# Prompt mixer of a two-layer hybrid decoder: five vector jobs of each tile done by POOL in place of DVE

## What is computed

```python
def rglru_mixer(...):                 # convolution, gates, recurrence
    u = conv_b
    for j in range(CONV_W):           # 4 taps
        u = u + xc[:, j:j + T] * conv_w[j]
    r = sigmoid(einsum(ub, rg_wa) + rg_ba); i = sigmoid(einsum(ub, rg_wx) + rg_bx)
    log_a = -RG_C * r * softplus(-rg_lambda)
    a = exp(log_a)
    b = sqrt(-expm1(2.0 * log_a)) * i * u          # 1 - a^2
    h = linear_scan(a, b, h0)
    y = gelu(a_gate) * h                           # the gate polynomial

q = partial_rope(rmsnorm(b_q per head, q_norm), pos)   # head squares
k = partial_rope(rmsnorm(b_k per head, k_norm), pos)

def index_scores(qi, wi, ki):         # decides which 256 keys a row attends to
    dots = einsum('bqhd,bsd->bqhs', qi, ki) * (IDX_DIM ** -0.5)
    return einsum('bqh,bqhs->bqs', wi, relu(dots))
```

## Time and profile before

| | us |
|---|---|
| median of three runs | 4593.22 (4589.61 to 4599.74) |
| the profiled execution | 4589.05, its span 4587.4 |
| prompt mixer, both layers, from the timeline | about 2 x 945 |
| PE busy over the span | 3712.4 (81%) |
| DVE busy | 2138.1 (47%) |
| ACT busy | 1037.1 (23%) |
| POOL busy | 546.9 (12%) |

### The profile page before, as it was taken

The page is one execution under the profiler, slowest core; times in us unless marked ns, Lnnn a source line. Parts: engine busy times, 40 slices in busy tenths (PEclk is TensorE's granted clock), DMA queues, the critical chain, the costliest instruction groups (busy, mean ns, idle before and its releaser), DMA issues.

```text
span 4587.4 us, 52594 instructions
## 1 busy us (share of the span) xinstructions
PE 3712.4 (81%) x17978; PEld 2757.6 (60%) x17978; DVE 2138.1 (47%) x4901; ACT 1037.1 (23%) x2273; POOL 546.9 (12%) x767
## 2 busy tenths in 40 slices
PE   5787778776638999999957787787766389999999
PEld 3555455553324899989835554554433248899898
DVE  1357788715503344344413577787155033443443
ACT  2322333223300211112022333332233002111120
POOL 0100100114120000100001000001141201001000
PEclk9888877556769999999978888775567699999999
DMA  3000000015331111111130000000153311111111
GB/s 121 19 13 14 14 10 8 7 29 168 98 130 60 46 37 56 37 37 56 44 120 20 12 13 15 10 8 7 30 170 96 128 60 47 37 56 37 37 56 49
DMA packets 165855, 230.68 MB, mean 50 GB/s; under 512 B 64562, under 2 KB 130164, under 8 KB 163540
## 3 DMA queue, kind: packets, MB, share of 16 engines
q1 hardware_dynamic: 139892, 166.03, 11.0%
q0 software_dynamic: 25696, 61.29, 4.4%
HBM read 203.74 MB, written 23.50 MB: 50 GB/s over the span
## 4 chain that ended last, share of the span: by engine, by line
PE 62%; issue 11%; DVE 10%; SPq 5%; ACT 4%; DVEq 2%; DMA 2%; POOLq 2%; POOL 1%; ACTq 0%
PE bank L1302 11%; PE bank L1303 11%; PE bank L1304 11%; PE bank L1012 9%; PE bank L1008 4%; PE bank L1110 3%; PE bank L1294 3%; DVE arena L1363 3%; SPq L455 2%; SPq L471 2%; ACT arena L642 1%; PE bank L1094 1%; POOLq L591 1%; DVE arena L1629 1%; SPq L424 1%
## 5 line engine op out<-in xcount | busy, mean ns | idle before, releaser
L1771 DVE TENSOR_TENSOR x_and_hraw<-x_and_hraw,bank 128x512 f32<-128x512 f32 (+1 forms) x576 | 396.4, 688 | 630.6 <-PE bank L1304 630.6
L642 ACT ACTIVATE arena<-bank 128x512 f32<-128x512 f32 (+11 forms) x926 | 356.2, 428 | 1112.6 <-PE bank L1012 335.8
L1012 PE MATMUL bank<-arena 128*128 128x512 f32 (+5 forms) x1440 | 526.3, 521 | 3.5 <-ACT arena L669 2.0
L1363 DVE TENSOR_SCALAR_CACHE_REDUCE arena<-arena,vectors 128x384 bf16<-128x384 f32 (+6 forms) x434 | 500.2, 1152 | 34.4 <-issue 2.5
L1302 PE MATMUL bank<-xT_hi,w_up_hi 128*128 128x364 f32 (+1 forms) x1536 | 506.7, 330 | 3.2 <-DVE vectors L1752 3.2
L1303 PE MATMUL bank<-xT_lo,w_up_hi 128*128 128x364 f32 (+1 forms) x1536 | 506.6, 330 | 0.0
L1304 PE MATMUL bank<-xT_hi,w_up_lo 128*128 128x364 f32 (+1 forms) x1536 | 506.5, 330 | 0.0
L1302 PE MATMUL bank<-w_down_hi,hidden_hi 128*128 128x512 f32 x1152 | 450.4, 391 | 7.5 <-issue 7.5
L1303 PE MATMUL bank<-w_down_lo,hidden_hi 128*128 128x512 f32 x1152 | 449.8, 390 | 0.0
L1304 PE MATMUL bank<-w_down_hi,hidden_lo 128*128 128x512 f32 x1152 | 449.6, 390 | 0.0
L1012 PEld LDWEIGHTS bank<-arena 128*128 128x128 f32 (+1 forms) x1440 | 254.4, 194 | 255.3 <-issue 225.4
(11 more groups left out here) (248 smaller groups left out, 4554.6 us busy)
## 6 DMA issues: line engine op xcount, KB each, us to landing
arena<-in_cache_k SPq DMA_DIRECT2D x256, 128.0 KB, 2.2
arena<-in_cache_v POOLq DMA_DIRECT2D x256, 128.0 KB, 2.4
w_up_landing<-in_w_up SPq DMA_DIRECT2D x32, 1024.0 KB, 7.5
w_down_landing<-in_w_down SPq DMA_DIRECT2D x32, 1024.0 KB, 4.9
arena<-in_w_in SPq DMA_DIRECT2D x16, 1322.0 KB, 17.6
out_projection<-in_w_out SPq DMA_DIRECT2D x16, 512.0 KB, 7.1
out_projection<-y_scratch SPq DMA_DIRECT2D x16, 512.0 KB, 3.6
y_scratch<-arena POOLq DMA_DIRECT2D x18, 256.0 KB
```

The source lines that it names most:

```text
L642: return act.activation(dst, src, ACT.Copy, scale=scale)
L1012: ins = mm(b[:R, o:o + w], xnT[:, c, 0:R], w_in[:, c, c0:c0 + w], start=c == 0, stop=c == 7)
L1363: ts(junk, sc, cf[:R].bitcast(F32), None, ALU.is_ge, ALU.add, accum_out=cnt[:R])
L1771: tt(x, x, b[P - R:P, :], ALU.add).then_inc(s_took, 1)
```

## The change

Five functions go from DVE's program into POOL's: `head_squares`, `conv`, `gelu_inner`, `one_minus_a2` and `index_scores`. POOL does the first three one after the other at the start of a stage, ahead of `rstd(s+1)`; `one_minus_a2` behind the issues of the key and value stores; the index scores of all chunks after that. DVE's reduction over 64 columns becomes six additions of halves on POOL, and each multiply-and-add of DVE (one instruction) becomes a multiply by a column of constants and an addition (two), with an area `taps` for what lies between. A new semaphore `s_scored` tells DVE's `top_sign` that the scores of its tile are complete; `recurrence` now waits for `s_u` itself. DVE keeps the two memsets of the sample tile, in `sample_states`. `stored(s_ybst)`, which used to follow the store of the attention output at once, comes after `stored(s_kst)`, and that comes after `one_minus_a2`. PE's, ACT's and SP's programs are unchanged.

```diff
+                def head_squares(t):
+                    R = rows(t)
+                    pool.wait_ge(s_evac, A_AT[l, t, "G2"] + 1)
+                    pool.tensor_tensor(sq[:R], hb[:R, 0:12, :], hb[:R, 0:12, :], ALU.mult)
+                    pool.drain()
+                    for w in (32, 16, 8, 4, 2):
+                        pool.tensor_tensor(sq[:R, :, 0:w], sq[:R, :, 0:w], sq[:R, :, w:2 * w], ALU.add)
+                        pool.drain()
+                    pool.tensor_tensor(small[:R, 32:44], sq[:R, :, 0], sq[:R, :, 1], ALU.add)
+                    pool.drain()
+                    inv_root(small[:R, 20:32], small[:R, 32:44], 1.0 / 64).then_inc(s_krs, 1)
...
+                def conv(t):
...
+                    for h in range(2):
...
+                        pool.tensor_scalar(uo, xs(0), convw[:, 0, h:h + 1], vecs[:, h:h + 1], ALU.mult, ALU.add)
+                        for j in range(1, 4):
+                            pool.tensor_scalar(tap[j % 2], xs(j), convw[:, j, h:h + 1], None, ALU.mult)
+                            pool.drain()
+                            ins = pool.tensor_tensor(uo, uo, tap[j % 2], ALU.add)
+                        pool.drain()
+                    pool.sem_inc(s_u, 1)
...
+                def index_scores(t, c):
...
+                            pool.tensor_scalar(src, src, wi, None, ALU.mult)
+                            pool.drain()
+                            pool.tensor_tensor(dst, dst, src, ALU.add).then_inc(s_idx, 1)
+                        pool.drain()
...
                     if s < TILES:
                         t, R = s, rows(s)
-                        pool.wait_ge(s_kssq, T(l, t) + 1)
-                        inv_root(small[:R, 20:32], small[:R, 32:44], 1.0 / 64).then_inc(s_krs, 1)
+                        head_squares(t)
+                        conv(t)
+                        gelu_inner(t)
                     if s + 1 < TILES:
                         rstd(s + 1)
...
+                        one_minus_a2(t)
                         stored(s_kst)
+                        if attends(s - 1) is not None:
+                            stored(s_ybst)
+                        if 2 <= t < NT:
+                            for c in range(len(chunks(width(t)))):
+                                index_scores(t, c)
                         pool.wait_ge(s_ossq, T(l, t) + 1)
...
-                        if h == 0 and P_:
-                            head_squares(s)
                         if h == 1:
-                            if P_:
-                                conv(s)
+                            if s == NT:
+                                sample_states()
                             if N_:
                                 norm_x(s + 1)
-                        if h == 2 and P_:
-                            gelu_inner(s)
...
-                        if h == 2 and P_:
-                            one_minus_a2(s)
...
-                        if h in (4, 5) and 2 <= s < NT and h - 4 < len(chunks(width(s))):
-                            index_scores(s, h - 4)
```

More of the change, by code:

```diff
@@ new lines, in one_minus_a2 @@
+                def one_minus_a2(t):
+                    R = rows(t)
+                    pool.wait_ge(s_thr, T(l, t) + 1)
+                    pool.tensor_tensor(hh[:, :, 0:R], la[:, :, 0:R], la[:, :, 0:R], ALU.mult)
+                    pool.drain()
+                    pool.tensor_scalar(hh[:, :, 0:R], hh[:, :, 0:R], 1.0, None, ALU.add)
+                    pool.drain()
+                    pool.tensor_tensor(b2[:, :, 0:R], b2[:, :, 0:R], hh[:, :, 0:R], ALU.mult)
+                    pool.drain()
+                    pool.tensor_scalar(b2[:, :, 0:R], b2[:, :, 0:R], 1e-18, None, ALU.max).then_inc(s_b2, 1)
@@ new lines, in index_scores @@
+                def index_scores(t, c):
+                    c0, w = chunks(width(t))[c]
+                    for i in range(4):
+                        pool.wait_ge(s_evac, A_AT[l, t, f"i{c}.{i}"] + 1)
+                        src, dst = rl[:, (IDX0[l, t] + 4 * c + i) % 2, 0:w], score[:, t % 3, c0:c0 + w]
+                        wi = wca[:, t % 2, i:i + 1]
+                        if i == 0:
+                            pool.tensor_scalar(dst, src, wi, None, ALU.mult).then_inc(s_idx, 1)
+                        else:
+                            pool.tensor_scalar(src, src, wi, None, ALU.mult)
+                            pool.drain()
+                            pool.tensor_tensor(dst, dst, src, ALU.add).then_inc(s_idx, 1)
+                        pool.drain()
+                    if c == len(chunks(width(t))) - 1:
+                        d = score[:, t % 3, t * P:(t + 1) * P]
+                        pool.tensor_tensor(d, d, cs("bias"), ALU.add).then_inc(s_scored, 1)
@@ L540, in _ @@
+                pool.wait_ge(s_w, NW * 16 * (l + 1))
                 rstd(0)
```

82 lines of the change are left out of this document (23 added, 59 removed).

## The result

The changed kernel takes 4724.48 us (median of four runs, 4720.35 to 4727.32) against 4595.67 for the kernel before in the same four rounds. The ratio is 1.0281, with an interval of 1.0263 to 1.0299. The profiled execution is at 4723.3 us, 134 us above the one of before. The forecast was slower, 4686 us, with a range up to 4775; the direction and the place were right, and the loss came out about 40 us larger than the sum.

The account below looks back on a forecast made before the run. PE was taken to bound each stage's body, behind a serial head that POOL's chain would lengthen. Terms gave +46.6 us a layer, +93 for two; 4589.05 became 4682, plus 4.2 for the median: 4686 us, range 4605 to 4775.

Parts of the forecast that it names:

- The bound: Prompt mixer stages 1 to 7: serial head, then body set by PE; only shortening the head shortens the stage.
- the port in full and somewhat dearer operations: Outcome band 4710 to 4770 us: POOL fully waits out DVE neighbours and its operations cost somewhat more; chance 0.20.
- the port in full: Rival: beside `heads`, POOL operations wait out DVE neighbours fully, +1.7 us per stage, 4713; chance 0.20 together with dearer operations.
- The chain on POOL: Stage head: squares, root, convolution, polynomial and `rstd` in series before `norm_x`, 19.6 us; 17 to 21 us had chance 0.42.
- eight with one input (0.31 each): POOL's convolution: eight one-input operations at 0.31 us each, within its 6.5 us.
- The neighbour on DVE: POOL's convolution beside DVE's nine `heads` operations: 2 us added for disturbance, between 0 and 3.7.
- the dear rival: POOL fixed costs of 0.4 us per operation, chain 25 to 29 us, 4833 at 28.8; dearer still had chance 0.11.
- What costs nothing: Stage body: 1 - a^2 (about 2.6 us) and index scores (14 us) on POOL are covered; up to +36 if not.
- 2.3 expected: Stage 7, head 6: PE's 2.26 us wait for ACT, behind DVE's maximum, goes: -2.3 us.
- 4.5 us of relief: Stage 8, where DVE sets the pace: convolution (2.5 us), polynomial and 1 - a^2 (2.0 us) leave its path.
- POOL is free at 787.97 + 2.3: Stage 8 head: norms there 8.1 us after POOL is free, 798.4 against 797.19, +1.2 us.
- The marks I had set: Signs in the trace: POOL releases `heads` and `norm_x`; PE's wait for `heads` 4 us longer in stage 1, about 1 in stage 6.

Follow-up runs that it names:

- body_only: Changed kernel with squares, convolution and gate polynomial back on DVE, only 1 - a^2 and index scores on POOL; 4583.12 us, ratio 0.9966.
- head_only: Changed kernel with 1 - a^2 and index scores back on DVE, only squares, convolution and gate polynomial on POOL; 4725.63 us, ratio 1.0271.
- conv_waits: Changed kernel in which POOL waits for DVE's `heads` to end before its convolution; 4750.04 us, ratio 1.0333.
- early_root: Kernel before, POOL taking the next tile's head root before the last store and waiting for stores behind `rstd`; 4571.29 us, ratio 0.9948.
- the last three: early_root plus 1 - a^2 and two-operation index scores on POOL; then also convolution and polynomial behind `rstd` from tile 5, or 3: 4554.91, 4545.47, 4547.52 us.

## Why the prediction was right, and where its sum was short

**The bound, right.** A stage is a serial head and a body that PE sets. The body of stage 6 kept its length to 0.2 us, and `body_only` and `head_only` put all of the loss in the head. The measured time lies in the range, but not in the part of it (4645 to 4710) that my chain gave: it lies in the next one, to which I had given 0.20 for the port in full and somewhat dearer operations. Dearer operations came true, the port in full did not, and about half of what the sum was short has other reasons, told below.

**The chain on POOL, right in kind, 1.4 us short.** Forecast 19.6 us, measured 21.0. By its parts in stage 1: squares 5.2 (5.3 forecast), root 2.8 (2.8), polynomial 2.1 (2.1), `rstd` 0.9 (0.9), and the convolution 9.8 against 6.5 + 2. The term that failed is "eight with one input (0.31 each)". The six taps that only multiply take 0.6 us each undisturbed, which is 1.7 us more in all; I had priced them like the small ones with two operations. The neighbour on DVE cost 1.6, not 2. Over seven stages the norm's shift is 9.8 us above the forecast, which is these 1.4 us on the mean. Stage by stage it is 0.2 to 2.5: POOL got free 1.2 us sooner in stage 6, and 1.2 us later in stage 7, behind the start of the stage than I had read from the kernel before. The test that I had named, a one-input operation of 128 columns at over 0.5 us, came out on the side of the dear rival; but it holds for one form only and the chain stayed in the band of 17 to 21 us. The price was uneven over the forms, which no row of before could show for more than twelve columns.

**The port in full, refuted in stage 1.** 1.6 of 3.7 us, as the rows of `conv_waits` show; its total alone could not have told.

**"What costs nothing", right about the covers; the clock was left at nothing.** The index multiply took 1.56 us, for which I had 0.6, and its cover held all the same: `conv_waits` has it and no excess. The bodies of stages 1 to 6 still make +5.6 us in layer 0 and +2.5 in layer 1. The term behind it is one that I had named and given no number, PE at a lower granted clock: PE is busy for 8.2 and 7.4 us more per layer with the same matmuls. In stage 7 the body gave 3.2 and 3.0 us, 2.3 expected.

**Stage 8, wrong by 5.2 us in layer 0 and by 2.3 in layer 1.** I had its heads 1.2 us later and 4.5 us of relief. In layer 1 they are 1.4 us later and the stage is 1.0 us shorter, so only the relief fell short there. In layer 0 they are 3.9 us later, since POOL is free only here (timeline of POOL in the changed kernel):

```profile
851.19 0.54 POOL L518 DMA_DIRECT2D y_scratch<-arena  x1 [7.89 <-ACT arena L717]
857.67 1.46 POOL L544 TENSOR_TENSOR arena<-arena 64x768 f32<-64x768 f32 x1 [5.94 <-DMA y_scratch<-arena]
...
866.02 1.16 POOL L570 TENSOR_SCALAR arena<-arena 128x64 f32<-128x64 f32 x1
```

POOL waits for all its stores, not for `yC` alone, and the last ones of the convolution's state, single elements, were issued shortly before (timelines of POOL, the changed kernel's and then the one of before):

```profile
841.98 0.75 POOL L518 DMA_DIRECT2D out_conv_prompt<-arena  x1
```

```profile
775.10 0.75 POOL L517 DMA_DIRECT2D out_conv_prompt<-arena  x1
```

The wait ends 15.7 us behind that issue now (857.67), and it ended 15.2 us behind it before (790.31). In layer 0 of nine kernels (all but `early_root` and the last three, whose POOL doesn't wait there) it ends 14.8 to 16.3 us behind it, while it ends anything from 2.3 to 6.9 us behind the store of `yC`; in layer 1, where this wait ended it, 12.3 to 13.3 us. So it is most likely this store that lands last. "POOL is free at 787.97 + 2.3" was right for the kernel before, where `yC` follows 12.9 us behind that issue and both would land at about the same time. In the changed kernel `yC` follows only 9.2 us behind it, and the wait comes out. Of the relief only 2.0 us showed (3.9 later, the stage 1.9 longer): DVE got free sooner and then waited for PE's logits.

```profile
866.04 0.95 DVE L1491 TENSOR_TENSOR arena<-arena,vectors 64x768 f32<-64x768 f32 x1 [5.05 <-POOL vectors L525]
...
883.62 0.69 DVE L1648 CUSTOM_DVE_ANT_0 arena<-bank,arena 128x512 f32<-128x512 f32 x1 [1.64 <-PE bank L1185]
```

**The books.** Layer 0: norm in stages 1 to 7 +9.8, stage 0 +0.6, bodies +5.6 less the 0.9 more that stage 7 gave, stage 8 +5.2: 20.3 us. Layer 1: norm +12.5, stage 0 +1.5, bodies +2.5 less 0.7, stage 8 +2.3: 18.1 us. With 2 us outside the mixers that is the 41 us that the sum was short (134 - 93). About 20 of them are the chain's price (1.4 us in 14 stages); the rest is PE's pace, stage 8 and the start of the stages.

**The marks I had set.** `heads` and `norm_x` are released by POOL in every stage, as said. PE's wait for `heads` grew by 5.7 us in stage 1 (10.71 to 16.37) where I had said 4, and by 1.9 in stage 6 (12.32 to 14.20) where I had said 1. By my own price of the squares, 5.3 us that all stand ahead of `heads`, stage 1 should have read 5: DVE's squares had cost the head nothing there. The rest is `heads` itself, held by the convolution beside it (4.47 us from its start to its end, 3.92 before).

**What stays open.** Why `body_only` is 1.6 us shorter in stage 0 of layer 0 and not in layer 1, no run tells. That stages 1 and 2 grew by 0.9 and 0.4 us more than `norm_x` was late, and that `body_only` is longer by 1 us there and by 2 us in stage 4, goes with PE's busy time (48.7 and 48.6 us in stage 1, 47.6 before), but the clock was never varied by itself. In the second stretch of stage 6 the granted clock is 0.57 (before 0.50) while the stretch is longer.

## What to carry to other kernels

Ask not which engine is busy but which chain of small steps ends last at the start of a stage; work that goes into such a chain costs its full length there, even on an engine that is idle for 88% of the span, and work that comes out of it, as in `early_root`, pays without moving a job. When several results are made in a row on one engine, make the one that is waited for first: that alone gave back 90 of the 129 us. The same move can be good or bad by what stands around it: the convolution on POOL loses ahead of `rstd`, and behind it, without the squares, it gains from tile 3 or 5 on (earlier tiles weren't tried in that form). And before a difference of 2 us in one stage is given a cause, look whether the other layer has it too.

## What the runs showed of the hardware

- POOL's `TENSOR_SCALAR` with one operation costs about twice the form with two: 1563 against 697 ns for 128x512, 876 against 407 for 128x256, 603 against 377 for 128x128. With maximum as the second operation it isn't so (1078 ns for 128x256). The Trainium skill (GPSIMD Engine Reference, section 4.1) calls one-input work on this engine roughly line-rate; here DVE does 128x1024 of it in 0.75 us, so even the cheap form, 697 ns for half of that, is nearly twice as slow.
- POOL's two-input operations: 1270 ns for 128x512, 1.46 us for 128x768.
- POOL and DVE hold each other off at the start of such a meeting (1.21 and 1.29 us for instructions of 0.45 and 0.63) and then take turns. DVE pays too: single instructions of `heads` took 0.55 us where they take 0.29.
- The stores of the convolution's state, single elements, seem to hold a wait for 14.8 to 16.3 us from their issue in layer 0 and 12.3 to 13.3 in layer 1, where one behind a 128x256 store alone lasts 2.2. That they are what it waits for is inferred from the agreement of the traces; no run left them out.
- The same 336 matmuls of stage 4 keep PE busy for 70.7 us at a mean granted clock of 0.87 (before, layer 0), 73.2 at 0.83 and 76.0 at 0.80 (`head_only`, layers 0 and 1).
